# A single-core transformer layer: two token tiles projected from resident weights inside tile 0's steps, instead of from weights read again at its end

## What is computed

```
proj = rms_norm(x, ln1) @ w_in          # 1024 x 2592: q, k, v, gate, c_q, c_kv, k_pe
ret  = retention over chunks of 64 (8 heads), its norm, times silu(gate)
mla  = attention (8 heads) on the latents c_kv and k_pe
h    = x + concat(ret, mla) @ w_o       # 1024 x 1024
q    = rms_norm(h, ln2) @ w_q           # 1024 x 2048
top_s, top_i = top_k(q . sub_keys, 16)  # 8 heads x 2 halves, 128 keys each
expert, g    = the best 16 of the 16 x 16 pairs of each head, and their softmax
a    = gelu(sum_d xn2 * u[expert]) * g  # 128 rows of u for each token
y    = rms_norm(h + sum a * v[expert], lnf)
```

## Time and profile before

| | us |
|---|---|
| median of 3 runs | 2223.96 |
| lowest and highest of the runs | 2219.17 and 2226.92 |
| the profiled execution, its own time | 2226.64 |
| its span on the core | 2224.8 |

### The profile page before, as it was taken

The page is one execution under the profiler, slowest core; times in us unless marked ns, Lnnn a source line. Parts: engine busy times, 40 slices in busy tenths (PEclk is TensorE's granted clock), DMA queues, the critical chain, the costliest instruction groups (busy, mean ns, idle before and its releaser), DMA issues.

```text
span 2224.8 us, 18489 instructions
## 1 busy us (share of the span) xinstructions
PE 1772.5 (80%) x6517; PEld 744.1 (33%) x6517; DVE 1270.0 (57%) x2956; ACT 234.7 (11%) x506; POOL 1223.8 (55%) x1291
## 2 busy tenths in 40 slices
PE   6787948776798787987988866598897677777798
PEld 3555346442333342333333512143352111111122
DVE  1417778499754477455654795754468754454400
ACT  1221013100111011011111100011010000000000
POOL 0001425456677535446775455476655677767675
PEclk9579968899999988999999998799999999999999
DMA  7336959999999997979999999799999999999998
GB/s 271 114 98 230 355 199 344 383 347 334 410 409 409 409 406 297 411 300 411 409 409 410 404 360 364 241 399 400 409 409 396 364 409 409 409 410 410 409 408 340
DMA packets 233324, 796.35 MB, mean 358 GB/s; under 512 B 35312, under 2 KB 42352, under 8 KB 232144
## 3 DMA queue, kind: packets, MB, share of 16 engines
q0 software_dynamic: 185088, 681.79, 78.5%
q1 hardware_dynamic: 46416, 110.74, 13.4%
q10 hardware_dynamic: 1728, 2.65, 0.3%
HBM read 787.89 MB, written 7.19 MB: 357 GB/s over the span
## 4 chain that ended last, share of the span: by engine, by line
DMA 34%; PE 26%; DVE 21%; POOL 13%; issue 6%; ACT 1%; SPq 0%; ACTq 0%; DVEq 0%; POOLq 0%
DMA rows<-in_u,eidx 15%; DMA rows<-in_v,pair_idx 11%; PE acc L847 9%; DVE rows L1442 7%; POOL rows L530 7%; POOL rows L541 6%; PE F L585 4%; PE F L790 3%; DMA wblk<-in_w_q 2%; DMA wblk<-in_w_in 2%; DMA keys_all<-in_state 1%; DMA wblk<-in_w_o 1%; PE F L764 1%; DVE work L1349 1%; PE acc L562 1%
## 5 line engine op out<-in xcount | busy, mean ns | idle before, releaser
L847 PE MATMUL acc<-rows,spread_w 128*32 128x512 f32 x2560 | 978.4, 615 | 245.8 <-DMA rows<-in_v,pair_idx 243.2
L1442 DVE CUSTOM_DVE_ANT_0 rows<-rows,xps 128x1024 f32<-128x1024 f32 x640 | 767.7, 1219 | 524.7 <-DMA rows<-in_u,eidx 522.4
L530 POOL DMA_INDIRECT rows<-in_u,eidx x640 | 605.9, 947 | 674.3 <-DVE dots L1442 363.5
L541 POOL DMA_INDIRECT rows<-in_v,pair_idx x640 | 612.5, 957 | 283.4 <-issue 157.7
L847 PEld LDWEIGHTS acc<-rows,spread_w 128*32 128x32 f32 x2560 | 201.6, 111 | 942.4 <-DMA rows<-in_v,pair_idx 544.7
L790 PE MATMUL F<-work,wblk 128*128 128x128 f32 x1280 | 162.3, 285 | 17.5 <-DMA wblk<-in_w_q 14.6
L790 PEld LDWEIGHTS F<-work,wblk 128*128 128x128 f32 x1280 | 152.6, 198 | 46.9 <-issue 25.1
L585 PE MATMUL F<-wblk,work 128*128 128x512 f32 (+1 forms) x384 | 151.5, 550 | 14.3 <-ACT work L938 9.2
L585 PEld LDWEIGHTS F<-wblk,work 128*128 128x128 f32 x384 | 67.4, 192 | 100.1 <-issue 76.6
L764 PE MATMUL F<-wblk,work 128*128 128x512 f32 x160 | 79.3, 635 | 15.0 <-DMA wblk<-in_w_o 13.7
L1448 DVE TENSOR_SCALAR stat<-stat 128x1 f32<-128x1 f32 x5 | 0.8, 154 | 116.3 <-ACT ybuf L1084 116.3
(11 more groups left out here) (204 smaller groups left out, 1231.6 us busy)
## 6 DMA issues: line engine op xcount, KB each, us to landing
wblk<-in_w_q SPq DMA_DIRECT2D x80, 512.0 KB, 6.9
wblk<-in_w_o SPq DMA_DIRECT2D x40, 512.0 KB, 7.2
wblk<-in_w_in SPq DMA_DIRECT2D x40, 512.0 KB, 7.0
rows<-in_w_in POOLq DMA_DIRECT2D x5, 2048.0 KB, 9.1
rows<-in_u,eidx POOLq DMA_INDIRECT x640, 11.2
rows<-in_v,pair_idx POOLq DMA_INDIRECT x640, 11.1
work<-proj_d SPq DMA_DIRECT2D x2, 1296.0 KB, 10.9
hbuf<-in_x_all SPq DMA_DIRECT2D x5, 512.0 KB, 7.9
```

Source lines behind the costliest of these rows:

```text
L530: nc.gpsimd.indirect_dma_start(urow[n % U_SLOTS], None, a["u"], bass.IndirectOffsetOnAxis(eidx[:, t % 2, pick:pick + 1], 0)).then_inc(u_in ...
L541: nc.gpsimd.indirect_dma_start(vrow[n % V_SLOTS], None, a["v"], bass.IndirectOffsetOnAxis(pair_idx[:, t % 2, item:item + 1], 0)).then_inc( ...
L847: last = mm(acc[ROPE * (i % 4):ROPE * (i % 4) + ROPE, 512 * c:512 * c + 512], spread_w[:, at:at + ROPE], vrow[q % V_SLOTS][:, 512 * c:512 ...
L1442: v.tensor_tensor_reduce(urow[n % U_SLOTS], urow[n % U_SLOTS], xps[:, :], 1.0, 0.0, ALU.mult, ALU.add, dots[:, g % 2, k:k + 1]).then_inc(d ...
```

## The change

Tiles 1 and 2 are no longer projected at tile 0's boundary. Instead, while tile 0's own steps run, PE multiplies the `w_in` blocks that lie in the `win` buffers (2, 3, 4 and the narrow one, still there from tile 0's projection) with tile 1 and with tile 2, and then the blocks 0 and 1, which POOL loads a second time. This makes 12 more items (block, tile) of 8 matmuls, cut into 24 halves of 4 matmuls; 20 of the halves are 512 columns wide and 4 are 32 columns wide. `beside_first` spreads them evenly over tile 0's steps up to `query` 7. ACT evicts every item to a stage in `spread_w` and stores it to `proj_d` with a DMA of its own queue; SP loads tile 1's projection from there after tile 0's `w_q`, and tile 2's in tile 1. The rows of all tiles for the first norm are loaded earlier, and ACT squares them before tile 0's turn_qk instead of in its query. POOL's first gather also waits for all items and stores and for the clearing of `spread_w`. Tile 0's boundary keeps only the picking steps and 4 units; `ENDS` goes from 13 to 4 for tile 0 and from 56 to 57 for tile 1. The pair at tile 2's boundary stays as it was.

```diff
-PAIRED = (0, 2)
+PAIRED = (2,)
...
-ENDS = (13, 56, 122, 185, 249)
-EARLY = ((("pairs", 1), ("best", 3), ("places", 1), ("gates", 1))
-         + tuple(("project", b) for b in range(IN_BLOCKS - 9, IN_BLOCKS)))
+ENDS = (4, 57, 122, 185, 249)
+EARLY = (("pairs", 1), ("best", 3), ("places", 1), ("gates", 1))
...
+        xt = [three(flat_rows[:, 12288:13312], KD), three(flat_rows[:, 13312:15360], KD)]
+        win.append(three(wv(PJ + IN_COLS, KD * ROPE), KD))
+        first_stage = three(spread_w[:, 0:2 * 512], 2)
+        sq_junk = spread_w[:, D_MODEL:2 * D_MODEL]
+        xs = [wv(R, D_MODEL), hbuf[:, 0, :], hbuf[:, 1, :], xn2[:, :], ybuf[:, :]]
         xt_pair = three(wv(R, 2 * D_MODEL), KD)
         stage = three(wv(R + 2 * D_MODEL, 2 * 512), 2)
...
-        loads = [(0, 0), (1, 1), (2, 2), (3, 0), (4, 1), (5, 3)]
-        NIN = len(loads)
+        loads = [(0, 0), (1, 1), (2, 2), (3, 0), (4, 1), (5, 3), (0, 2), (1, 0)]
+        second = [(2, 2), (3, 0), (4, 1), (5, 3), (0, 2), (1, 0)]
+        items = [(cb, buf, 0) for cb, buf in loads[0:6]] + [(cb, buf, t) for cb, buf in second for t in (1, 2)]
+        NIN = len(items)
+        last_beside = [name for name, i, _ in steps_of(0)].index("query") + HEADS - 1
+        halves = 2 * (NIN - 6)
+        def beside_first(step):
+            at = [halves * min(k, last_beside + 1) // (last_beside + 1) for k in (step, step + 1)]
+            return [(6 + m // 2, m % 2) for m in range(at[0], at[1])]
         banks = [acc[:, 0:512], acc[:, 512:1024], xps[:, 0:512], xps[:, 512:1024]]
         width = [512] * 5 + [ROPE]
...
-            sp.wait_ge(mm_in, 4)
+            sp.wait_ge(mm_in, 2)
+            sp.dma_start(xt[1], a["x_t"][:, :, P:3 * P]).then_inc(xt_in[1], 16)
             for t in range(1, TILES):
                 sp.dma_start(xs[t], a["x_all"][P * t:P * t + P, :]).then_inc(xs_in[1], 16)
-            sp.wait_ge(mm_in, NIN)
+            sp.wait_ge(mm_in, 6)
             for dst, name in ((gnw, "gn"), (q_prompt, "q_prompt"), (qnw, "qn"), (kvw, "kvn"), (s_decay, "s_decay"),
...
+                else:
+                    sp.wait_ge(sq_done, TILES)
                 sp.dma_start(hbuf[:, t % 2, :], a["x_all"][P * t:P * t + P, :]).then_inc(xres_in, 16)
+                if t == 1:
+                    sp.dma_start(pj, proj_d[1]).then_inc(pj_in, 16)
                 if t - 1 in PAIRED:
                     for i in range(2):
-                        sp.wait_ge(stored[i], 48 * (t // 2 + 1))
-                    sp.dma_start(pj, proj_d[t // 2]).then_inc(pj_in, 16)
+                        sp.wait_ge(stored[i], 48)
+                    sp.dma_start(pj, proj_d[2]).then_inc(pj_in, 16)
...
+                if t == 0:
+                    for i in range(2):
+                        sp.wait_ge(first_stored[i], 16 * (NIN - 6) // 2)
+                    sp.dma_start(pj, proj_d[0]).then_inc(pj_in, 16)
...
-            for cb, buf in loads:
-                if cb in (3, 4):
-                    pool.wait_ge(mm_in, cb - 2)
+            for n, (cb, buf) in enumerate(loads):
+                if n in (3, 4):
+                    pool.wait_ge(mm_in, n - 2)
+                elif n >= 6:
+                    pool.wait_ge(mm_in, 6 + 2 * (n - 5))
                 src = a["w_in"][cb] if cb < 5 else a["w_in_pe"]
                 pool.dma_start(win[buf].rearrange("p k n -> p (k n)"), src).then_inc(win_in[buf], 16)
-            nc.gpsimd.memset(spread_w[:, :], 0.0).then_inc(spread_zero, 1)
             pool.wait_ge(mm_in, NIN)
             pool.wait_ge(sq_done, TILES)
+            for i in range(2):
+                pool.wait_ge(first_stored[i], 16 * (NIN - 6) // 2)
+            nc.gpsimd.memset(spread_w[:, :], 0.0).then_inc(spread_zero, 1)
...
+            def project_first(n, half):
+                cb, buf, t = items[n]
+                if half == 0:
+                    load = n if n < 6 else n // 2 - 1
+                    pe.wait_ge(win_in[buf], 16 * sum(b == buf for _, b in loads[0:load + 1]))
+                    pe.wait_ge(xt_ok, KD if t == 0 else 2 * KD)
+                    if n >= 4:
+                        pe.wait_ge(ev_in, n - 3)
+                for k in range(KD // 2 * half, KD // 2 * half + KD // 2):
+                    lhs = xt[0][:, k, :] if t == 0 else xt[1][:, k, P * (t - 1):P * t]
+                    last = mm(banks[n % 4][:, 0:width[cb]], lhs, win[buf][:, k, :], start=(k == 0), stop=(k == KD - 1))
+                if half == 1:
+                    last.then_inc(mm_in, 1)
+            for n in range(6):
+                for half in range(2):
+                    project_first(n, half)
             pe.wait_ge(consts_in[0], 16 * 5)
...
             def run_units(t, step):
+                if t == 0:
+                    for n, half in beside_first(step):
+                        project_first(n, half)
                 for number in unit_span(t, step):
...
+            def project_first(n):
+                cb, _, t = items[n]
+                w, i = width[cb], n % 2
+                act.wait_ge(mm_in, n + 1)
+                if n >= 8:
+                    act.wait_ge(first_stored[i], 16 * ((n - 6) // 2))
+                dst = pj[:, 512 * cb:512 * cb + w] if t == 0 else first_stage[:, i, 0:w]
+                nc.scalar.activation(dst, banks[n % 4][:, 0:w], ACT.Copy, scale=rstd1[:, t:t + 1]).then_inc(ev_in, 1)
+                if t >= 1:
+                    act.wait_ge(ev_in, n + 1)
+                    act.dma_start(proj_d[t - 1, :, 512 * cb:512 * cb + w], dst).then_inc(first_stored[i], 16)
+            for n in range(6):
+                project_first(n)
+            token_roots(1, TILES)
+            act.wait_ge(rstd1_ok, 2)
...
             def run_units(t, step):
+                if t == 0:
+                    for n, half in beside_first(step):
+                        if half == 1:
+                            project_first(n)
                 for number in unit_span(t, step):
                     unit(number)
...
-            dve.wait_ge(xt_in[0], 32)
-            for k in range(KD):
-                v.tensor_scalar(xt[:, k, :], xt[:, k, :], ln1[:, k:k + 1], None, ALU.mult).then_inc(xt_ok, 1)
+            def scale_xt(i):
+                dve.wait_ge(xt_in[i], (32, 16)[i])
+                for k in range(KD):
+                    v.tensor_scalar(xt[i][:, k, :], xt[i][:, k, :], ln1[:, k:k + 1], None, ALU.mult).then_inc(xt_ok, 1)
...
+            scale_xt(0)
             token_roots(0, 1)
+            scale_xt(1)
             dve.wait_ge(consts_in[0], 16 * 5)
...
                 if t == 0:
-                    dve.wait_ge(ev_in, NIN)
+                    dve.wait_ge(ev_in, 6)
                 elif t - 1 in PAIRED:
                     dve.wait_ge(picks_ok, PARTS * t)
-                    dve.wait_ge(ev_pj, 12 * (t // 2 + 1))
+                    dve.wait_ge(ev_pj, 12)
                 else:
                     dve.wait_ge(picks_ok, PARTS * t)
-                    dve.wait_ge(pj_in, 16 * (t // 2))
+                    dve.wait_ge(pj_in, 16 * min(t, 3))
                 rotate(qk, pj[:, 0:1024], rtmp, cos64[:, t, :], sin64[:, t, :], 2 * HEADS, HD // 2
...
                     if step == "rotate":
                         rotate_qk(t)
+                        if t == 0:
+                            token_roots(1, TILES)
                     elif step == "ret_scores":
```

More of the change, by code:

```diff
@@ L199, in sem @@
             return ctx.enter_context(nc.semaphore(name))
-        proj_d = nc.dram_tensor("proj_d", (len(PAIRED), P, IN_COLS), F32, kind="Internal").ap()
+        proj_d = nc.dram_tensor("proj_d", (3, P, IN_COLS), F32, kind="Internal").ap()
         rows = sb("rows", [P, U_SLOTS + V_SLOTS, D_MODEL])
@@ L261, in build @@
         win = [three(flat_rows[:, 4096 * i:4096 * i + 4096], KD) for i in range(3)]
-        xt = three(flat_rows[:, 12288:13312], KD)
-        win.append(three(flat_rows[:, 13312:13312 + KD * ROPE], KD))
-        sq_junk = flat_rows[:, 13568:13568 + D_MODEL]
-        xs = [wv(R, D_MODEL)] + [flat_rows[:, D_MODEL * i:D_MODEL * i + D_MODEL] for i in range(SAMPLE)]
+        xt = [three(flat_rows[:, 12288:13312], KD), three(flat_rows[:, 13312:15360], KD)]
[3 more added lines that the diff above has]
+        xs = [wv(R, D_MODEL), hbuf[:, 0, :], hbuf[:, 1, :], xn2[:, :], ybuf[:, :]]
         xt_pair = three(wv(R, 2 * D_MODEL), KD)
@@ L594, in turn_qk @@
                 if t - 1 in PAIRED:
-                    pe.wait_ge(ev_pj, 12 * (t // 2 + 1))
+                    pe.wait_ge(ev_pj, 12)
                 for g in range(4):
@@ L927, in _ @@
             act.wait_ge(rstd1_ok, 1)
-            for cb in range(NIN):
-                act.wait_ge(mm_in, cb + 1)
-                nc.scalar.activation(pj[:, 512 * cb:512 * cb + width[cb]], banks[cb % 4][:, 0:width[cb]], ACT.Copy,
-                                     scale=rstd1[:, 0:1]).then_inc(ev_in, 1)
+            def project_first(n):
[13 more added lines that the diff above has]
+            act.wait_ge(rstd1_ok, 2)
```

(4 more changed lines are left out.)

36 lines of the change are left out of this document (12 added, 24 removed).

## The result

| | before | after |
|---|---|---|
| median, us | 2226.92 (5 runs) | 2239.76 (5 runs) |
| lowest and highest | 2219.17, 2229.17 | 2238.13, 2240.62 |
| profiled execution; its span | 2226.64; 2224.8 | 2238.13; 2236.3 |
| moved by DMA, MB | 796.35 | 792.58 |

The ratio is 1.0063 [1.0044, 1.0082]: slower by 0.6%, in the range and near the forecast.

A forecast was written before the change was run, and what follows sets the result against it. Expert work was taken as bound by the rate at which DMA brings rows. Tile 1's start -2.1, tile 1 +18.0 and the rest -5.1 sum to +10.8: profiled 2237.4 us, median 2235, range 2214 to 2255.

The forecast's parts named there:

- up to `turn_c`: Tile 0's lead-in: three halves lie in PE's wait of 13.98 us, one ahead of `ret_scores` costs time; +1.2 us.
- attention up to `w_o`: Tile 0's lead-in: halves and waits on ACT cost 17.2 + 2.8 + 5.0, a full clock saves 15.2; +9.8 us.
- residual and norm: Tile 0's lead-in: ACT's eviction, store and table load ahead of the square root make 4.7 us 11.2; +6.5.
- `turn_x2` and half: Tile 0's lead-in: the transpose and the half behind it, both after a PE pause; +4.3 us.
- queries: Tile 0's lead-in, up to the key scores: two halves cost 6.9 us, a slow start goes away; +5.2 us.
- tile 1's start: Lead-in 37.0 us longer, boundary without the projection: tile 1 starts at 285.1 instead of 287.2; -2.1 us.
- tile 1: Its length with 53 units for 43: 20 more dots, four units hidden on DVE; +18.0 us, bounds 12 and 25.7.
- the rest: From tile 2's start to the end: 57 units done instead of 56, four gathers fewer for full DMA engines; -5.1 us.
- The cheap lead-in: Rival: ACT's evictions and table load hide, lead-in costs 22 to 25 us, time 2217; chance 0.19.
- Bytes are not the time: Judges the rival that DMA engines are the bound: 3.8 MB less, 9.2 us less, time 2215; chance 0.08.
- The low clock: Rival: the clock stays low in tile 0's attention, +15.2 us, time 2250; chance 0.12.
- The two sides did not cancel: Judges the rival that the two sides cancel: lead-in about 28 us, time 2226; chance 0.09.

The follow-up runs named there:

- before_wide: The kernel before with 22 unused wide matmuls, two at each of tile 0's eleven attention steps; 2222.97 us, ratio 0.9997.
- short_halves: The changed kernel with one matmul of four in tile 2's halves, its projection incomplete, evictions and stores kept; 2215.64 us, ratio 0.9969 to the kernel before.
- norm_order: The changed kernel with ACT's square root of the second norm ahead of the item's eviction and store; 2231.49 us, ratio 1.0039 to the kernel before.
- norm_wide: norm_order with 7 unused wide matmuls in TensorE's waits in tile 1's attention; 2224.54 us, ratio 1.0013 to the kernel before.
- boundary: norm_order with eight items in the lead-in, halves moved to TensorE's waits, and four items behind tile 0's last key scores; 2205.43 us, ratio 0.9919 to the kernel before.
- boundary_warm: boundary with unused wide matmuls in tile 1's attention, ahead of both tiles' turn_qk and ahead of tile 1's turn_c; 2199.67 us, ratio 0.9905 to the kernel before.
- boundary_few: boundary_warm with 2 units instead of 4 in tile 0's boundary; 2206.18 us, ratio 0.9936 to the kernel before.

## Why the prediction held, point by point

The forecast for the profiled execution was 2237.4, and it took 2238.1. The median is 4.8 above the 2235 forecast; I had taken 2.7 off for the way the kernel before stood to its median of three runs, and the changed kernel's median lies 1.6 above its profile. Over five runs the kernel before stands 0.3 above its own: the 2.7 was no property of it.

| step of the prediction | forecast | measured |
|---|---|---|
| up to `turn_c` | +1.2 | -0.5 |
| to the first scores | +9.3 | +10.3 |
| attention up to `w_o` | +9.8 | +14.1 |
| `w_o` | +0.7 | -0.1 |
| residual and norm | +6.5 | +6.6 |
| `turn_x2` and half | +4.3 | +4.7 |
| queries | +5.2 | +4.1 |
| lead-in together | +37.0 | +39.3 |
| tile 1's start | -2.1 | +0.1 |
| tile 1 | +18.0 | +16.5 |
| the rest | -5.1 | -5.1 |
| sum | +10.8 | +11.5 |

From the key scores to the picks it took 0.8 more than before, and from the picks to tile 1's rotation 40.9, against 0.8 and 40.8 forecast. That the sum is met to 0.7 is in part luck: attention came 4.3 dearer than forecast, the steps up to `turn_c` and the queries 1.7 and 1.1 cheaper, and tile 1 1.5 shorter. The signs came as named: key scores done at 220.4 (218 forecast), picks at 246.4 (244), a PE wait of 4.25 with the table load in it, tile 1 at 287.3 (285), tile 2 at 549.0 (548), a DMA share of 0.99 from there on.

- **Attention.** The mechanism held: with the wide halves the clock was 0.93 up to the last head and 0.83 up to `w_o`, and before_wide shows by itself that such work gives back 16.2, where 15.2 stood in the sum. The 5 for waits on ACT came as 2.06 and 1.57. What the sum missed is the end: I let the clock stay high up to `w_o`, but behind the last wide half only narrow halves and small matmuls follow, and `values_up` ran at 0.50 again. That is 3.3 for L774, 0.9 for the transposes and 1.7 for the narrow halves, 1.4 of which the shorter waits made good. Why the clock fell there is open: in short_halves the same steps stood behind even less wide work, and `values_up` took 3.76.
- **Norm.** Right in size and cause: norm_order takes the 4.25 away. Its consequence for the clock, 3.0 more, stood in my 4.3 for the transpose and half, though I put it down to a pause and not to ACT's order.
- **Tile 1.** The size is right and the make-up wrong, so this term is met by luck. Twenty dots cost 11.0 with the old lead-in, just under my bound of 12: more than four units hide. The other 5.5 are the clock at `values_up` and `w_o` of tile 1, which I had not considered at all; norm_wide gives it back.
- **The rest.** That -5.1 is met to the tenth is luck: over the ten kernels that have 57 units at tile 1's end and their full projection the rest takes 1687.2 to 1692.0, 1689.2 on average, against 1692.4 and 1692.7 with 56.
- **Rivals.** The cheap lead-in falls (second key scores at 219, not 206). Bytes are not the time: 3.8 MB less, 11.5 us more. The low clock came mainly in the last 11 of attention's 49 us. The two sides did not cancel.

## What to carry to other kernels

Before moving work into a gap, ask what runs beside it where it stands: the projection at the boundary was half hidden by DVE's picks, and taking all of it out left TensorE idle for those 40 us while the lead-in, where all wait for TensorE, paid 39. Put into such a stretch only what its waits, and a clock that the work brings back, pay for (in boundary 16 halves, 12 x 3.43 + 4 x 0.95 = 45 us of matmuls, made the second key scores 4.4 later than in the kernel before), and leave the rest where it was hidden. Where an in-order engine evicts for two streams, let the short step that others wait for go first: at the norm this gave 4.25 us and 3.0 more by the clock. And read the granted clock stage by stage: a stage that runs at 0.5 can be worth more than the work that was moved.

## What the runs showed of the hardware

- Work that nobody reads made kernels faster: 7 matmuls of 128x512 in TensorE's waits gave 5.6 us in one tile, 30 gave 10 us in all. The 22 of before_wide cost what they gave (ratio 0.9997): they stood where TensorE had no wait.
- TensorE's granted clock was 0.53 in a stretch in which it was busy 93% of the time with small matmuls, and 1.00 with wide ones between them (before_wide).
- The clock is not a function of the instructions alone. boundary_warm and boundary_few have the same ones up to the last key scores, start their first matmul 1.2 us apart, and differ by 8 us there; L612 and L621 took half as long in before_wide as in before. What decides it at such a place stays open, and a difference of a few us between two single executions is no evidence by itself.
- A start that is earlier by 29 us gave 19 at the end in short_halves, but 35.5 gave 32.9 in boundary. In short_halves' tile 1 DVE waited 2.9 more for the copies of the key scores, 0.9 more for `w_o` and 0.6 more for rows than in the changed kernel, which makes up its 4.4; what delayed these, and the 5.5 of the rest, was not tried.
